# A chunked delta-rule scan inside a two-block network on one core: small tasks moved between engines, stages and places in the order

## The reference, cut to what matters

```python
def _wkv_step(S, inp):
    r_t, w_t, k_t, v_t, a_t, b_t = inp
    sa = jnp.einsum('zbhvk,zbhk->zbhv', S, a_t)
    S = S * w_t[..., None, :] + sa[..., :, None] * b_t[..., None, :] + v_t[..., :, None] * k_t[..., None, :]
    return S, jnp.einsum('zbhvk,zbhk->zbhv', S, r_t)

def rwkv_out(y, h, xx, r, k_mod, v, mu, ln_g, ln_b, r_k, g1, g2, wo):
    ...
    bonus = jnp.einsum('bthk,zbthk->bth', _heads(r) * r_k, _heads(k_mod))
    y = y.astype(r.dtype) + bonus[..., None] * _heads(v)
    xg = h + xx * mu[5]
    gate = jax.nn.sigmoid(xg @ g1) @ g2
    return (y.reshape(bsz, n, d) * gate) @ wo

def swiglu(h, w_gate, w_up, w_down):
    return (jax.nn.silu(h @ w_gate) * (h @ w_up)) @ w_down
```

## Time and profile before

| | us |
|---|---|
| three runs, median | 4273.11 |
| three runs, lowest and highest | 4266.0 and 4274.78 |
| the profiled execution, its own time | 4270.57 |
| its span in the profile | 4268.7 |
| granted TensorE clock, share of full speed, mean | 0.919 |

### The profile page before, as it was taken

One profiled execution on the slowest core, in us unless ns is written; L12 is line 12 of the kernel. 1 busy time (PEld: TensorE's weight loads), 2 busy tenths in 40 slices (PEclk: granted clock), 3 DMA queues, 4 the chain that ended last, 5 costly groups with the idle time before them and its releaser, 6 DMA issues. The chain is left out here.

```text
span 4268.7 us, 78087 instructions
## 1 busy us (share of the span) xinstructions
PE 3578.3 (84%) x31346; PEld 2529.4 (59%) x31346; DVE 2075.6 (49%) x3273; ACT 1243.7 (29%) x2681; POOL 1361.4 (32%) x1069
## 2 busy tenths in 40 slices
PE   8889999998999999977778758976889887587774
PEld 6667877556878787762222227736888886422221
DVE  4559963548992455560000017627788884400002
ACT  3342223443223322321111112233445453111112
POOL 4444443443444454730000013404545451000001
PEclk9989999999999999979898889997999997798987
DMA  4115442213542222549999982543322223499997
GB/s 126 48 64 183 177 149 74 73 50 138 177 165 95 89 74 82 175 161 379 421 421 421 421 347 78 181 162 83 78 57 75 77 54 144 186 413 427 426 426 295
DMA packets 245738, 819.09 MB, mean 192 GB/s; under 512 B 61336, under 2 KB 68840, under 8 KB 185680
## 3 DMA queue, kind: packets, MB, share of 16 engines
q1 hardware_dynamic: 236960, 786.13, 49.3%
q0 software_dynamic: 7920, 28.84, 1.7%
q10 hardware_dynamic: 576, 0.09, 0.0%
HBM read 738.84 MB, written 76.12 MB: 191 GB/s over the span
## 5 line engine op out<-in xcount | busy, mean ns | idle before, releaser
L2819 POOL DMA_INDIRECT moe0e_xg<-moe_h,moe_first_rows x19 | 18.0, 947 | 594.0 <-DMA moe_first_rows<-moe_table 543.4
L3767 PE MATMUL scan_bank<-scan_T,scan_off 64*64 64x64 f32 x3840 | 163.4, 224 | 40.9 <-issue 34.4
L1218 DVE SCALAR_TENSOR_TENSOR f1u_ada<-hT,condition,f1u_ada 128x512 f32<-128x512 f32 x168 | 196.8, 1240 | 0.2 <-DVE f1u_ada L1218 0.2
L2851 PE MATMUL moe0e_p_g<-moe_ring,moe0e_xT 128*64 128x512 f32 x608 | 174.6, 652 | 17.9 <-issue 9.2
L2819 POOL DMA_INDIRECT moe1e_xg<-moe_h,moe_first_rows x16 | 15.0, 939 | 539.6 <-DMA moe_first_rows<-moe_table 453.8
L3491 POOL TENSOR_TENSOR scan_off<-scan_pairs,scan_join 128x256 f32<-128x256 f32 x240 | 181.0, 790 | 0.0
L1218 DVE SCALAR_TENSOR_TENSOR f0u_ada<-hT,condition,f0u_ada 128x512 f32<-128x512 f32 x168 | 171.7, 1091 | 2.9 <-DMA hT<-in_ada_w_dram 2.6
L365 POOL TENSOR_TENSOR gmi_w_lo<-gmi_rows_w,gmi_w_hi 128x512 fp32r<-128x512 f32 x64 | 120.2, 1878 | 162.7 <-ACT gmi_w_hi L407 162.7
L3767 PEld LDWEIGHTS scan_bank<-scan_T,scan_off 64*64 64x64 f32 x3840 | 140.8, 138 | 48.6 <-issue 40.4
L2851 PE MATMUL moe0e_p_u<-moe_ring,moe0e_xT 128*64 128x512 f32 x608 | 168.6, 631 | 0.0
L365 POOL TENSOR_TENSOR p_w_lo<-p_rows_w,p_w_hi 128x512 fp32r<-128x512 f32 (+3 forms) x88 | 113.5, 1292 | 163.9 <-ACT p_w_hi L407 163.9
(11 more groups left out here) (741 smaller groups left out, 10406.8 us busy)
## 6 DMA issues: line engine op xcount, KB each, us to landing
moe_ring<-in_moe_w_gu_dram SPq DMA_DIRECT2D x280, 1024.0 KB, 21.6
moe_ring<-in_moe_w_down_dram SPq DMA_DIRECT2D x140, 1024.0 KB, 22.3
hT<-in_ada_w_dram SPq DMA_DIRECT2D x48, 1024.0 KB, 6.4
f0u_w<-in_ffn_w_gate_up_dram SPq DMA_DIRECT2D x22, 1024.0 KB, 4.8
f1u_w<-in_ffn_w_gate_up_dram SPq DMA_DIRECT2D x22, 1024.0 KB, 4.8
gmi_rows_w<-in_ga_w_in_dram SPq DMA_DIRECT2D x64, 256.0 KB, 2.8
gmo_w<-in_ga_w_out_dram SPq DMA_DIRECT2D x64, 256.0 KB, 3.0
p_rows_w<-in_ab_w_in_dram SPq DMA_DIRECT2D x48, 256.0 KB, 2.7
```

What stands on the lines that cost most here:

```text
L1218: ins = V.scalar_tensor_tensor(out=acc[:, z, :], in0=src, scalar=cond[:, n * HALF + k, z:z + 1], in1=acc[:, z, :], op0=ALU.mult, op1=ALU.add)
L2819: pool.indirect_dma_start(xg[:], None, H.h, bass.IndirectOffsetOnAxis(rows[:, 0:1], 0)).then_inc(gathered, 16)
L2851: mm = nc.tensor.matmul(p[r, :], xT[:, kd, r], ring[:, s, half, k, g * HID:(g + 1) * HID], start=(kd == 0), stop=(kd == KD - 1), skip_grou ...
L3767: mm = nc.tensor.matmul(out[r], lhsT[r], rhs[r], start=start, stop=stop, skip_group_check=True)
```

## The change

- In the scan, ScalarE makes the high half of the block after the second step of the walk, in front of the copies of the turned matrices, instead of behind round 11. VectorE makes the bonus rows, the low half and the addition of the offset, in this order, between the copy of the bonus sums and round 0. POOL makes neither the low half nor the offset any more. The offset needs one buffer instead of two. SyncE stores the halves and loads the next raw block and offsets before it waits for y and loads v.
- `project_split` leaves the last job's stores out where the caller gave `stored`; the gates' stage issues them behind its four weight loads. The semaphores of these stores and of the first weights are cleared at the end of the gates' stage.
- In the up projections VectorE's first multiplication stands in front of the first half of the second sum.

```diff
@@ project_split, SyncE
-                store(len(jobs) - 1)
+                if not later:
+                    store(len(jobs) - 1)
@@ swiglu_up, VectorE
                 split_sum(0, True)
+                multiply(0, 0)
                 add_half(1, 0)
-                multiply(0, 0)
                 add_half(1, 1)
@@ rwkv_scan, SyncE: body
+                    sp.wait_ge(s["lo_made"], h + 1)
+                    for d, w in zip(wo, (w_hi, w_lo)):
+                        sp.dma_start(block_of(d, h), w[:].bitcast(F32)).then_inc(s["w_stored"], 16)
+                    if ahead is not None:
+                        sp.wait_ge(s["bonus_shifted"], h + 1)
+                        load_raw(ahead)
                     if walk is not None:
                         sp.wait_ge(s["y_copied"], walk + 1)
                         if ahead is not None:
                             load_v(ahead)
-                    sp.wait_ge(s["bonus_done"], h + 1)
-                    sp.wait_ge(s["lo_made"], h + 1)
-                    for d, w in zip(wo, (w_hi, w_lo)):
-                        sp.dma_start(block_of(d, h), w[:].bitcast(F32)).then_inc(s["w_stored"], 16)
-                    if ahead is not None:
-                        if h:
-                            sp.wait_ge(s["bonus_shifted"], h)
-                        load_raw(ahead)
@@ POOL: body
-                    pool.wait_ge(s["hi_made"], h + 1)
-                    nc.gpsimd.tensor_tensor(w_lo[:], w_raw[:], w_hi[:], ALU.subtract).then_inc(s["lo_made"], 1)
-                    if h:
-                        add_shift(h - 1)
@@ ScalarE: body
                     walk_both(1)
+                    act.wait_ge(s["raw_loaded"], 32 * h + 32)
+                    act.wait_ge(s["w_stored"], 32 * h)
+                    A(w_hi[:], w_raw[:], ACT.Copy).then_inc(s["hi_made"], 1)
                     copy_turned(0)
...
-                        if n == NZ - 4:
-                            act.wait_ge(s["raw_loaded"], 32 * h + 32)
-                            act.wait_ge(s["w_stored"], 32 * h)
-                            A(w_hi[:], w_raw[:], ACT.Copy).then_inc(s["hi_made"], 1)
@@ VectorE: body
+                    def add_shift():
+                        hs = slice(h * HK, h * HK + HK)
+                        dve.wait_ge(s["bonus_done"], h + 1)
+                        V.tensor_tensor(bonus_rows[:, :, hs], bonus_rows[:, :, hs], shift[:].rearrange("p (o c) -> p o c", o=1).broadcast_to([P, NT, HK]),
+                                        ALU.add).then_inc(s["bonus_shifted"], 1)
+
+                    def split_block():
+                        dve.wait_ge(s["hi_made"], h + 1)
+                        V.tensor_tensor(w_lo[:], w_raw[:], w_hi[:], ALU.subtract).then_inc(s["lo_made"], 1)
+
+                    add_bonus()
+                    split_block()
+                    add_shift()
                     if ahead is not None:
                         fc = Chain(dve, s["factor_step"], ahead * FACTOR_STEPS)
                     for n in range(NZ):
...
-                        if n == NZ - 2:
-                            add_bonus()
@@ rwkv_gates
+    pending, last_stores = pending
...
+        st.sems += [first_loaded] + [stored for stored, _ in pending]
@@ rwkv_gates, SyncE, behind the four weight loads
+                for dst, src in last_stores:
+                    sp.dma_start(dst, src).then_inc(pending[-1][0], 16)
@@ rwkv
-            pending = [(stored[u], 16 * sum(len(job["stores"]) for job in jobs[u::2])) for u in range(2)]
+            pending = [(stored[u], 16 * sum(len(job["stores"]) for job in jobs[u::2])) for u in range(2)], jobs[-1]["stores"]
```

More of the change, by code:

```diff
@@ L3357, in rwkv_scan @@
         w_raw, w_hi, w_lo = sb("w_raw", [P, BANK]), sb("w_hi", [P, BANK], F32R), sb("w_lo", [P, BANK], F32R)
-        shift = [sb(f"shift{u}", [P, HK]) for u in range(2)]
+        shift = sb("shift", [P, HK])
         bon = sb("bonus", [P, NT])
@@ L3430, in load_raw @@
                     sp.dma_start(w_raw[:], block_of(a["rw_wo_2"], h)).then_inc(s["raw_loaded"], 16)
-                    sp.dma_start(shift[h % 2][:], a["rw_ln_b_2"][h * HK:h * HK + HK].partition_broadcast(P)).then_inc(s["raw_loaded"], 16)
+                    sp.dma_start(shift[:], a["rw_ln_b_2"][h * HK:h * HK + HK].partition_broadcast(P)).then_inc(s["raw_loaded"], 16)
                 def body(h, walk, ahead):
@@ L3493, in body @@
                         factors(ahead)
-                    pool.wait_ge(s["hi_made"], h + 1)
-                    nc.gpsimd.tensor_tensor(w_lo[:], w_raw[:], w_hi[:], ALU.subtract).then_inc(s["lo_made"], 1)
-                    if h:
-                        add_shift(h - 1)
-                def add_shift(h):
-                    hs = slice(h * HK, h * HK + HK)
-                    pool.wait_ge(s["bonus_done"], h + 1)
-                    nc.gpsimd.tensor_tensor(bonus_rows[:, :, hs], bonus_rows[:, :, hs],
-                                            shift[h % 2][:].rearrange("p (o c) -> p o c", o=1).broadcast_to([P, NT, HK]), ALU.add).then_inc(s["bonus_shifted"], 1)
                 factors(0)
                 heads(body)
-                add_shift(LAST)
             @block.scalar
```

## The result

The changed kernel takes 4231.81 us (median of 4 runs, 4227.45 to 4233.24) beside 4273.24 for the kernel before (4 runs): 41 us less, ratio 0.9905, 95% interval 0.9887 to 0.9922. I had forecast 4255 with a range of 4242 to 4267. Its profiled execution took 4233.24 us, span 4231.3, against 4270.57 and 4268.7, so the two traces are 37.4 us apart.

A forecast was written before the change was run, and what follows sets the result against it. TensorE's stream was taken to set the pace, held up by VectorE in places. Stores -10.9, scan -7 and up projections 0 gave -18 us against the profiled 4270.57, so 4252.6, or 4255 us for the median; range 4242 to 4267.

The forecast's parts named there:

- Part 1, the stores: End of the value projections: issuing the last 13 stores in the gates' stage removes the engines' wait, gaining 10.9 us.
- rival "Slower": Scan: late VectorE lengthens TensorE's mid-head waits and drops it to 1.2 GHz; +11 us, 4284 us, chance 0.05.
- Part 2, the boundary: Scan, between heads: without the bonus products there, TensorE's wait for the fourteenth addition to R goes, -13.2 us.
- VectorE's lateness and POOL's list: Scan: moved operations delay VectorE before the first Z·R product, +7 us, and push out POOL's 15 products, +3 us.
- the sum of eight shortfalls: Scan: VectorE's gap before the first Z·R product is under 4.2 us in eight of 16 heads; shortfalls sum to 8.6 us.
- My sentence on the Trainium skill, SBUF - State Buffer, "Who interferes with whom": Scan: by the exclusion rule alone the four moved operations would take 4.3 us; the identity's additions don't bear it out.
- SyncE's order: Scan: two stores, raw block and offset row leave the boundary's burst, 0.8 of 2.7 MB; -4 us, bounds -15 and +8.
- 21 us in such disturbances: Scan: 15 heads lose 1.4 us each against undisturbed head 7, read as TensorE's instructions late behind bulk transfers.
- rival "the burst was the cost": Scan: with 0.8 MB less in the boundary's burst most late instructions go, 12 us more gain; 4243 us, chance 0.14.
- Part 3, the up projections: Up projections: TensorE's 5.31 us wait only moves behind the third unit; 0 us, bounds -4 and +2.

The follow-up runs named there:

- e5: Kernel before, with only VectorE's two bonus products moved ahead of round 0, before the first Z·R product: 4257.07 us, ratio 0.9973.
- e2: Kernel before, with only SyncE's order changed: block stores, next raw block and offset row issued mid-head instead of at the boundary: 4258.5 us, ratio 0.9976.
- e3: Kernel before, with only the last value stores moved into the gates' stage: 4250.87 us, ratio 0.9965.
- e4: Kernel before, with only the first multiplication of the up projections moved ahead of the eight modulation terms: 4268.75 us, ratio 0.9999.
- e9: Changed kernel, plus two 384 KB stores a head to spare DRAM that nothing waits for, issued at the boundary: 4236.33 us, ratio 0.9925.
- e10: Changed kernel, plus two 384 KB stores a head to spare DRAM that nothing waits for, issued mid-head: 4233.0 us, ratio 0.9908.
- e13: Changed kernel, with loads of k and a held until the head's first turn and r loaded mid-head behind the raw block: 4235.75 us, ratio 0.9923.
- e14: Kernel before with the edits of e2, e3, e4 and e5, plus the load spreading of e13: 4226.6 us, ratio 0.9908.

## Why the prediction was wrong

**Part 1, the stores: right.** 10.9 us at the seam, exactly. The reason that I gave held (nothing else held the gates' stage). Left out were the 3.5 us of the gates' stage, most of them the granted clock of 0.50 after the long wait. I had cited a row with such a clock in the scan and did not ask what the clock was behind the 11.21 us wait. The rival "Slower" tied the clock to the length of a wait from that one row. The same trace does not bear it out: over the three microseconds behind a wait of 1.95 us that ends at 3252.29 the clock is 0.60, behind one of 2.75 us that ends at 3458.98 it is 1.00.

**Part 2, the boundary: right.** -13.2 forecast, -12.2 by the waits; e5 alone gained 11 by the ratio.

**VectorE's lateness and POOL's list: right in size, partly by luck.** +7 and +3 forecast. From mask to mask, TensorE's waits for `scan_off` and `scan_Sm` grew by 9.6 us. The four operations took 3.72 us against 4.2: the two-operand rate beside POOL was the row to take, not the 0.45 us of the identity's additions. POOL's 15 products of a head span 12.9 us in the mean where they spanned 11.3, 1.6 more against the 1.4 that I had. But I forecast that VectorE would still have idle time in about half of the heads, and it has none in any of the 16. The long gaps of the kernel before (up to 8.12 us) held TensorE's late instructions; with SyncE's order alone changed (e2) ten of the 16 gaps are 3.2 us or less and 13 no longer than 3.72. So the sum of eight shortfalls with operations of 4.2 us stood for a smaller shortfall in every head. My sentence on the Trainium skill, SBUF - State Buffer, "Who interferes with whom", stands as it did: the moved operations fit its exclusion (1.79, 1.10 and 0.95 us), the identity's additions, still 0.42 to 0.47 us beside the same POOL products, do not.

**SyncE's order: this step failed.** I put it at -4 us, with bounds of -15 and +8. The issue waits fell by 18.3 us in the changed kernel and by 15.3 in e2, which changes nothing else (by 15 and 12 against the profiles of e3 and e4, whose scan is the old one); in time e2 gained 10 us by the ratio (6 to 14). In the first 20 us of a head alone, where the transfers run, the issue waits sum to 16.1 to 19.3 us in the three profiles of the old scan, 9.1 in e2, and 6.1 and 6.8 in the two of the changed kernel: 9 to 13 us are there, and the rest of the 18.3 lies later in the head, with its cause open. The mechanism was right, and the row for its size stood in my text: 21 us in such disturbances. I gave them only a fifth of that by the share of bytes taken away, 0.8 of 2.7 MB, and by the thought that a head freed of this wait meets VectorE's shortfall instead. The share of bytes is no measure. As I read it, what matters is whether the transfers are still under way when TensorE needs its next piece of code; the four taken away let SyncE start the burst's last issue 5.0 to 6.5 us into a head, where it was 5.8 to 8.3, 1.5 us earlier in the mean. The rival "the burst was the cost" was nearest to the truth about the scan; at 4243 it too was short of the first group's time, by the clock in the gates' stage, by the 2.6 us of variation in the output projection, and by the rest of this term. The kernel before also happened to be profiled at the dear end, 616.5 us of masks beside 610.8 and 610.9.

The sum again with the measured terms, for the profiled execution: -10.9 - 3.5 - 23.7 and +0.7 elsewhere give -37.4, against my -18. The issue waits account for 14 of the 19 missing, the clock for 3.5. Of these 14 some 5 to 9 are shown to be the queue's, by the first 20 us of the heads and by e2's time.

The Trainium skill, Runtime: NRT & Kernel Launch, "Instruction fetch mechanics", has the fetch mostly hidden. The trace of the kernel before speaks against that here, as far as the packets tell. DMA queues in its head 6 (packets, MB, share of 16 engines), from the boundary to the start of TensorE's 2.90 us wait, and then the first 1.6 us of that wait:

```profile
q1 hardware_dynamic: 2168, 1.75, 74.7%
q14 instruction: 2, 0.02, 0.5%
```

```profile
q1 hardware_dynamic: 169, 0.41, 102.2%
q8 instruction: 1, 0.02, 4.9%
```

Queue q8 carries one packet of 16 KB every 4.5 us through the scan (the middle value of its steps); here none for 8.8 us, under 1.75 MB of other traffic, and one while TensorE stands, which begins 2.9 us before TensorE goes on. Over the scan such steps reached 9.9 us. The other waits agree. Over the 17 profiles there are 51 issue waits of 1 us or more in the first 20 us of a head, and every one ends 2.3 to 3.0 us after the start of a q8 packet; of the times from 5 to 15 us into a head of the kernel before, only 13% lie so. The 85 such waits later in a head end 1.3 to 6.3 us after one. That these packets are what TensorE waits for is still read from their times; what the experiments show is that bytes at this place bring the waits and bytes elsewhere do not.

**Part 3, the up projections: right.** e4 is at 0.9999 (0.9989 to 1.0008), and the wait moved to where I had put it, 5.88 us.

## What to carry to other kernels

TensorE's "issue" waits that come and go from one pass of a loop to the next, in the shadow of a burst of transfers, are priced by comparing a disturbed pass with an undisturbed one, not by the share of the bytes that is taken away. Before an operation is moved, ask which transfer now has to be there earlier for it, and whether the queue's order gives it that (the early split needs the early raw block). Where a long wait of TensorE goes, count the granted clock behind it too. A stage that the change does not touch can differ by 3 us between two profiles: look at it in the other runs before explaining it.

## What the runs showed of the hardware that I had not expected

Bulk transfers slow TensorE though it reads none of their data: two stores of 384 KB a head that nothing waits for raised its issue waits from 30 to 44 us when issued at the boundary, and to 34 when issued in the middle. Late instructions and a late VectorE don't add up: e9 has 10 us more of issue waits than e10 and is 3 to 7 us slower. Issue waits of 1 us and more beside these transfers ended 2.3 to 3.0 us after the start of a 16 KB packet of queue q8, 51 of 51. And some 30 us of "issue" in the scan stayed however the transfers were spread (30.7 and 29.2 us in e13 and e14); most of them stand more than 20 us into a head, where no bulk transfer runs, and what they are stays open. The granted clock did not follow the length of TensorE's wait: 0.60 behind 1.95 us, 1.00 behind 2.75 us in one trace.
